# State-space tables built ahead of the expert loop, parked in DRAM and reloaded

## The reference

```python
abr = mag * jnp.cos(li * dt)            # Abar, 64 groups x 64 states
abi = mag * jnp.sin(li * dt)
bbar_re = qr[..., None] * br - qi[..., None] * bim
bbar_im = qr[..., None] * bim + qi[..., None] * br
bu_re = jnp.einsum('blgh,gph->blgp', u, bbar_re)
bu_im = jnp.einsum('blgh,gph->blgp', u, bbar_im)
...                                     # x_t = Abar x_{t-1} + Bbar u_t
y = (jnp.einsum('ghp,blgp->blgh', c_re, xr)
     - jnp.einsum('ghp,blgp->blgh', c_im, xi))
y = y + d * h                           # then GELU and a gated output projection
```

## Time and profile before

| what | value |
|---|---|
| device time, median of 3 runs | 2999.33 us (2990.56 to 3006.65) |
| the profiled execution's own time | 2996.05 us |
| its span, first to last instruction | 2994.3 us |
| busy: PE, DVE, ACT, POOL | 89%, 68%, 45%, 9% of the span |
| matmuls' chain (share of the span on PE) | 77% |
| granted TensorE clock, mean | 0.934 of full speed |
| expert loop, 407 to 1558 us | PE 1138.5 of 1151 us busy, clock 0.99, 364 GB/s |
| 1558 to 1908 us | PE busy in about half |

### The profile page before, as it was taken

How to read it: one execution, slowest core, us unless ns; L and a number is a source line. 1 busy time by engine, 2 the same in 40 slices (tenths; PEclk the granted TensorE clock), 3 DMA queues, 4 the chain that set the end, 5 groups by cost and what they waited for, 6 DMA issues and landing times.

```text
span 2994.3 us, 34160 instructions
## 1 busy us (share of the span) xinstructions
PE 2655.8 (89%) x12072; PEld 2135.3 (71%) x12072; DVE 2021.4 (68%) x1948; ACT 1335.2 (45%) x1316; POOL 282.6 (9%) x337
## 2 busy tenths in 40 slices
PE   6988589999999999999974772789999999799997
PEld 4766468888888888888852362668888778588885
DVE  5764578999989999999959935656653354533433
ACT  4331257777777777777742221232222232322221
POOL 1230230000000000000007300001100000000000
PEclk9998589999999999999986866889999999999998
DMA  6741589999999999999963066317754423233332
GB/s 235 251 132 43 189 289 377 375 376 379 376 376 377 377 377 376 377 377 378 377 190 123 0 70 56 95 53 217 231 148 111 108 70 82 57 94 97 103 97 67
DMA packets 368686, 634.84 MB, mean 212 GB/s; under 512 B 45004, under 2 KB 238740, under 8 KB 368436
## 3 DMA queue, kind: packets, MB, share of 16 engines
q1 hardware_dynamic: 346196, 539.16, 54.5%
q0 software_dynamic: 17296, 76.03, 7.5%
q10 hardware_dynamic: 5136, 18.88, 1.5%
HBM read 609.97 MB, written 24.58 MB: 212 GB/s over the span
## 4 chain that ended last, share of the span: by engine, by line
PE 77%; DVE 12%; DMA 4%; ACT 2%; SPq 2%; issue 1%; POOL 1%; DVEq 0%; POOLq 0%; ACTq 0%
PE bank L2035 35%; PE bank L2235 11%; PE bank L2236 11%; PE bank L2241 11%; SPq L507 2%; PE bank L2023 1%; PE bank L2011 1%; PE bank L2018 1%; PE bank L1860 1%; DMA ring<-in_w_ada 1%; DVE work L1597 1%; DMA cb<-in_w_ada 1%; DMA ring<-k_dram 1%; DVE cb L1217 1%; DVE work L1596 1%
## 5 line engine op out<-in xcount | busy, mean ns | idle before, releaser
L1487 DVE TENSOR_TENSOR slot_lo<-ring,slot_hi 128x2048 fp32r<-128x2048 f32 x384 | 864.8, 2287 | 113.7 <-ACT slot_hi L909 113.6
L909 ACT ACTIVATE slot_hi<-ring 128x2048 fp32r<-128x2048 f32 x384 | 736.4, 1920 | 304.5 <-PE bank L2035 274.9
L2035 PE MATMUL bank<-slot_hi,xs_hi 128*128 128x512 f32 x1024 | 325.3, 399 | 0.0
L2035 PE MATMUL bank<-slot_hi,xs_lo 128*128 128x512 f32 x1024 | 317.5, 391 | 0.0
L2235 PE MATMUL bank<-h_hi,fin_hi 128*128 128x512 f32 x704 | 277.6, 394 | 22.6 <-ACT h_hi L1043 22.1
L2236 PE MATMUL bank<-h_hi,fin_lo 128*128 128x512 f32 x704 | 276.0, 392 | 0.0
L2035 PE MATMUL bank<-slot_lo,xs_hi 128*128 128x512 f32 x1024 | 275.7, 391 | 0.0
L2035 PEld LDWEIGHTS bank<-slot_hi,xs_hi 128*128 128x128 f32 x1024 | 188.8, 189 | 59.8 <-issue 23.9
L2035 PEld LDWEIGHTS bank<-slot_hi,xs_lo 128*128 128x128 f32 x1024 | 193.4, 189 | 41.5
L2035 PEld LDWEIGHTS bank<-slot_lo,xs_hi 128*128 128x128 f32 x1024 | 193.4, 189 | 40.4
L1084 ACT ACTIVATE fin_hi<-rows 128x1024 fp32r<-128x1024 f32 x88 | 88.2, 1052 | 220.8 <-DMA rows<-in_w_ffn_in 220.8
(11 more groups left out here) (431 smaller groups left out, 4297.9 us busy)
## 6 DMA issues: line engine op xcount, KB each, us to landing
ring<-in_expert_w_gate_up SPq DMA_DIRECT2D x256, 1024.0 KB, 7.0
ring<-in_expert_w_down SPq DMA_DIRECT2D x128, 1024.0 KB, 6.7
rows<-in_w_ffn_in SPq DMA_DIRECT2D x88, 512.0 KB, 5.0
work<-in_w_ada POOLq DMA_DIRECT2D x64, 384.0 KB, 4.0
cb<-in_w_ada POOLq DMA_DIRECT2D x48, 384.0 KB, 4.6
y_dram<-cb ACTq DMA_DIRECT2D x32, 512.0 KB, 7.2
work<-in_w_ffn_out SPq DMA_DIRECT2D x8, 1408.0 KB, 7.0
rows<-in_w_ffn_out SPq DMA_DIRECT2D x8, 1408.0 KB, 6.9
```

What stands on the lines that cost most here:

```text
L909: act.activation(hi_of(e, j), slot[q], ACT.Copy).then_inc(s_slot_hi, 1)
L1487: tt(slot_lo[:, q], slot[q], whole(hi_of(e, j)), ALU.subtract).then_inc(s_slot_lo, 1)
L2035: last = mm(ps[banks + n], x[:, k, :], (lo if lower else hi)[:, k, 512 * n:512 * (n + 1)], start=(begins and lower == 0 and k == 0 and x i ...
```

## The change

The tables are built in front of the expert loop. `m_b` and the powers are computed on POOL (the powers in three doubling steps with up to 256 columns, from `early_power`), C is loaded and transposed for a first time (`c_early`, `c_first`), PE transposes `m_b` behind the logits and forms the lag products in two halves around the token ids, ACT copies the transposes into free places (`m_w_parts`) and stores them to `m_w_dram`, and SP stores the lag table behind expert 0's last weights. Behind the loop `m_t` and `m_w` are loaded from DRAM. Waits are added for this: DVE waits for the slabs and for the zeros before its routing work, ACT for the powers and the stores, SP holds back expert 0's four down slots until the lag products are made (they use the same place in `ring`), and PE waits for the copies of the lag products before it uses that bank again. C is loaded a second time behind the loop, for `m_c`.

```diff
-COLS_PLE = COLS_ROUTE + 2 + KD
-COLS_XT = COLS_PLE + G // 4 + KD
+COLS_MB = COLS_ROUTE + G // 4
+COLS_PLE = COLS_MB + 2 + KD
+COLS_XT = COLS_PLE + KD
...
+        m_b = ring[:, 16384:24576].rearrange("p (g v h) -> p g v h", g=G, v=CH)
+        slab = [m_b[:, :, v, :] for v in range(CH)]
+        i_bbar = slab[0]
+        c_early = ring[:, 16384:17408].rearrange("p (t two n) -> p t two n", t=8, two=2)
+        c_first = work[:, 9216:10240].rearrange("p (g h) -> p g h", g=G)
+        m_w_parts = [(0, ca[:].rearrange("p k t -> p (k t)")), (4096, nat[:, 2048:4096]), (6144, work[:, 7680:9216]),
+                     (7680, work[:, 2048:2560])]
...
+            def load_c(rows_of, r):
+                for d in range(2):
+                    part = (r + d) % 2
+                    load(rows_of[:, :, d, :], a[f"ssm_c_{('re', 'im')[part]}_2"][0].rearrange("(t g) h n -> (g h) t n", t=8), s_c_in)
+            kd = k_dram.rearrange("h g v o -> h g (v o)")
+            sp.wait_ge(s_score_sb, HEADS * NT)
+            load_c(c_early, 0)
+            sp.wait_ge(s_power_ok, 1)
+            sp.wait_ge(s_y_ps, HEADS)
+            sp.wait_ge(s_b_in, 32)
+            for r in range(2):
+                for d in range(2):
+                    load(b_in[r][NS * d:NS * (d + 1)], b_dram[(r + d) % 2], s_b_in)
+            sp.dma_start(kd[:, :, 0:(CH - 1) * GC],
+                         k_zero.unsqueeze(1).broadcast_to([GC, G, (CH - 1) * GC])).then_inc(s_k_out, 16)
...
-            sp.wait_ge(s_hn_stored, 16)
+            sp.wait_ge(s_act_stored, 16)
             sp.wait_ge(s_cols_ready, COLS_ROUTE)
             for half in range(2):
                 load(bias_rows[E * half:E * (half + 1), :], a["expert_b_gate_up"][0], s_bias_in)
             load(down_bias, a["expert_b_down"][0], s_bias_in)
+            sp.wait_ge(s_k_ps, 1)
             for q in range(8, 12):
                 load_slot(q, 0)
+            sp.wait_ge(s_k_sb, 2)
+            for v in range(CH):
+                sp.dma_start(k_dram[:, :, 2 * CH - 2 - v, :], k_sb[GC * v:GC * (v + 1), :, :]).then_inc(s_k_out, 16)
             load_up(1, 1, 1)
...
+            sp.wait_ge(s_k_out, 16 * (CH + 1))
+            sp.wait_ge(s_more_done, 1)
+            for v in range(CH):
+                load(m_t[GC * v:GC * (v + 1), :, :], kd[:, :, (CH - 1 - v) * GC:(2 * CH - 1 - v) * GC], s_t_in)
+            sp.wait_ge(s_pgate_ready, 2 * NT)
+            sp.wait_ge(s_act_stored, 16 * len(m_w_parts) + 16)
+            load(m_w, m_w_dram.rearrange("p (g m) -> p g m", g=G), s_t_in)
...
-            kd = k_dram.rearrange("h g v o -> h g (v o)")
-            sp.wait_ge(s_k_sb, 3)
-            for v in range(CH):
-                sp.dma_start(k_dram[:, :, 2 * CH - 2 - v, :], k_sb[GC * v:GC * (v + 1), :, :]).then_inc(s_k_out, 16)
-            sp.dma_start(kd[:, :, 0:(CH - 1) * GC],
-                         k_zero.unsqueeze(1).broadcast_to([GC, G, (CH - 1) * GC])).then_inc(s_k_out, 16)
-            sp.wait_ge(s_k_out, 16 * (CH + 1))
-            for v in range(CH):
-                load(m_t[GC * v:GC * (v + 1), :, :], kd[:, :, (CH - 1 - v) * GC:(2 * CH - 1 - v) * GC], s_t_in)
...
+            pool.wait_ge(s_score_sb, 6 * NT + 1)
+            pool.wait_ge(s_par_ok, 1)
+            step(pool.memset(k_zero, 0.0))
+            for r in range(2):
+                step(pool.tensor_copy(early_power[r][:, 0], par[:, r, :]))
+            for n in (1, 2, 4):
+                xr, xi = [v[:, 0:n] for v in early_power]
+                ar, ai = [v[:, n - 1:n].broadcast_to([P, n, G]) for v in early_power]
+                t0, t1 = [v[:, 0:n * G].rearrange("p (v g) -> p v g", v=n) for v in power_t]
+                step(ptt(t0, xr, ar, ALU.mult))
+                step(ptt(t1, xi, ai, ALU.mult))
+                step(ptt(early_power[0][:, n:2 * n], t0, t1, ALU.subtract))
+                step(ptt(t0, xr, ai, ALU.mult))
+                step(ptt(t1, xi, ar, ALU.mult))
+                step(ptt(early_power[1][:, n:2 * n], t0, t1, ALU.add))
+            pool.sem_inc(s_power_ok, 1)
+            def wide_g(v):
+                return v.unsqueeze(2).broadcast_to([P, G, GC])
+            def turned(dst, x, y, z, w, op):
+                step(ptt(s5_ta[0], x, wide_g(z), ALU.mult))
+                step(ptt(s5_ta[1], y, wide_g(w), ALU.mult))
+                step(ptt(dst, s5_ta[0], s5_ta[1], op))
+            def power_slab(v):
+                turned(slab[v], slab[CH - 1], i_bbar, early_power[0][:, CH - 2 - v], early_power[1][:, CH - 2 - v], ALU.add)
+            def bbar_slabs():
+                pool.wait_ge(s_b_in, 96)
+                pool.wait_ge(s_ct_ps, 2)
+                sign = sm[:, 192:193]
+                step(pool.tensor_scalar(sign, token[:, 0:1], NS - 0.5, 2.0, ALU.is_gt, ALU.mult))
+                step(pool.tensor_scalar(sign, sign, -1.0, None, ALU.add))
+                step(pool.tensor_scalar(turn[:], par[:, 2:4, :], sign, None, ALU.mult))
+                turned(slab[CH - 1], b_in[0], b_in[1], par[:, 2, :], turn[:, 1, :], ALU.add)
+            pool.wait_ge(s_ret_ready, 1)
+            bbar_slabs()
+            turned(i_bbar, b_in[1], b_in[0], turn[:, 0, :], par[:, 3, :], ALU.subtract)
+            for v in range(CH - 2, -1, -1):
+                power_slab(v)
+            pool.sem_inc(s_b_ready, 1)
+            pool.wait_ge(s_nat_ready, 2 * NT)
+            for r in range(2):
+                step(pool.tensor_copy(power[:, r], early_power[r]))
+            pool.sem_inc(s_power_ok, 1)
             pool.wait_ge(s_bias_in, 48)
             up_bias = bias_rows.rearrange("e (f two) -> e f two", two=2)[:, :, 1]
             pool.tensor_scalar(up_bias, up_bias, 1.0, None, ALU.add).then_inc(s_bias_one, 1)
             pool.wait_ge(s_route_ok, 1)
-            pool.wait_ge(s_hn_stored, 16)
+            pool.wait_ge(s_act_stored, 16)
+            pool.wait_ge(s_act_stored, 16 * len(m_w_parts) + 16)
...
-            pool.wait_ge(s_b_in, 96)
-            step(pool.tensor_scalar(b_in[1][0:NS], b_in[1][0:NS], -1.0, None, ALU.mult))
-            pool.wait_ge(s_more_done, 1)
-            bbar = m_b[:, :, CH - 1, :]
-            turned(bbar, b_in[0], b_in[1], par[:, 2, :], par[:, 3, :], ALU.add)
-            turned(i_bbar, b_in[1], b_in[0], par[:, 2, :], par[:, 3, :], ALU.subtract)
-            pool.sem_inc(s_b_ready, 1)
-            for v in range(CH - 2, -1, -1):
-                turned(m_b[:, :, v, :], bbar, i_bbar, power[:, 0, CH - 2 - v, :], power[:, 1, CH - 2 - v, :], ALU.add)
-            pool.sem_inc(s_b_ready, 1)
-            pool.wait_ge(s_pproj_ready, 2 * NT)
-            pool.memset(k_zero, 0.0).then_inc(s_k_sb, 1)
...
+            act.wait_ge(s_log_ps, 1)
+            act.wait_ge(s_act_stored, 16)
+            act.wait_ge(s_power_ok, 2)
+            for first, part in m_w_parts:
+                for at in range(0, part.shape[1], 512):
+                    column(part[:, at:at + 512])
+                act.wait_ge(s_cols_taken, COLS_ROUTE + (first + part.shape[1]) // 512)
+                act.dma_start(m_w_dram[:, first:first + part.shape[1]], part).then_inc(s_act_stored, 16)
...
+            act.wait_ge(s_act_stored, 16 * len(m_w_parts) + 16)
             for j in range(LEAD):
                 split_high(0, j)
+            act.wait_ge(s_k_ps, 1)
+            for n in range(2):
+                act.activation(k_sb[:, GP * n:GP * (n + 1), :], ps[n].rearrange("p (g h) -> p g h", g=GP), ACT.Copy).then_inc(s_k_sb, 1)
...
+            dve.wait_ge(s_b_ready, 1)
+            dve.wait_ge(s_k_out, 16)
...
-                if b == 0:
-                    dve.wait_ge(s_k_out, 16 * (CH + 1))
...
+            pe.wait_ge(s_c_in, 32)
+            for q in range(2):
+                c_transposes(c_early, q, 6 + q)
...
+            pe.wait_ge(s_b_ready, 1)
+            for q in range(G // 4):
+                column([m_b[:, 4 * q + j].rearrange("p v h -> p (v h)") for j in range(4)])
+            def lag_kernels(half):
+                for g in range(GP * half, GP * (half + 1)):
+                    last = mm(ps[half][:, GC * (g % GP):GC * (g % GP + 1)], m_b[:, g].rearrange("p v h -> p (v h)"), c_first[:, g, :], start=True, stop=True)
+                return last
...
+            lag_kernels(0)
             for n in range(NT * TOPK):
                 pe.wait_ge(s_slot_hot, 2 * n + 2)
                 last = mm(ps[6][:, 0:TILES], row_hot[:, n, :], tile_token[:, n, :], start=(n == 0), stop=(n == NT * TOPK - 1))
             last.then_inc(s_ids_ps, 1)
+            lag_kernels(1).then_inc(s_k_ps, 1)
...
+            pe.wait_ge(s_k_sb, 2)
...
-            pe.wait_ge(s_pgate_act, 2 * NT)
-            for g in range(G):
-                last = mm(ps[g // GP][:, GC * (g % GP):GC * (g % GP + 1)], m_b[:, g].rearrange("p s h -> p (s h)"),
-                          s5c[0][:, g, :], start=True, stop=True)
-            last.then_inc(s_k_ps, 1)
...
-            pe.wait_ge(s_t_in, 16 * CH)
```

88 lines of the change are left out of this document (32 added, 56 removed).

## The result

The changed kernel takes 2951.64 us (median of 4 runs, 2943.95 to 2954.05); the kernel before, 3001.27 us in the same session (4 runs, 2990.56 to 3006.65). The ratio is 0.9835, 95% interval 0.9801 to 0.9868: faster by 1.65%, some 50 us. The profiled execution took 2949.81 us with a span of 2948.1, against 2996.05 and 2994.3. The forecast was 2952.

What follows compares the result with a forecast made beforehand. TensorE (PE) bounds the expert loop, so only the stretches around it count: -69.4 behind, +31.5 in front, -8 between the first experts, -45.9 us from 2996.05 to 2950; forecast 2952, range 2930 to 2980.

Steps and rivals of the forecast that it cites:

- the table's transposes: Behind the loop: the table's 64 transposes leave PE, net 1.0 us gained after 2.5 given back for a lower clock.
- Behind the loop, contention, -34.3: Behind the loop: without POOL's 27 operations DVE's work runs clean and the last projection pair ends 34.3 us earlier.
- Lag table's return, -34.1: Behind the loop: waits for the lag table's stores and return from DRAM go, first GELU starts 34.1 us earlier.
- m_w reload, nothing: Behind the loop: 4 MB of m_w come back in 11 us under 60 us of cover, so no cost.
- Slabs in front, +19.2: In front of the loop: POOL's 27 slab operations hold DVE's port, rows ready 19.2 us later; bounds 6 and 30.
- the 10 to 12 among my signs: Sign of being right: twelve tiny DVE operations take 10 to 12 us in front of the logits.
- the early lock is cheap: Rival: in front, POOL's operations slip between PE-paced ones; front costs 17 instead of 31.5, total 2937 us; chance 0.18.
- Columns between logits and ranks, +5.0: In front: 16 transpose groups and ACT copies delay DVE's reading of the ranks by 5.0 us; bounds 2 and 12.
- Second half of the lag products, +7.3: In front of expert 0: the second half of 64 lag products holds up PE, 7.3 us; bounds 3 and 14.
- Between experts 0 and 1, -8: Token tile 1's gather no longer queues behind the powers, less later weight loads: 8 us gained; bounds 0 and 11.
- ACT waiting for weights in experts 0 to 2: Sign of being wrong: in the loop's first experts, ACT waits for weights; no size given.
- the second: Rival: front costs 44, the gather's 8 us gain is lost, late loads stall ACT's splits; 2972 us, chance 0.20.

Runs made afterwards that it cites:

- experiment 3: The kernel before without POOL's 27 table operations behind the loop, all else kept: 2966.92 us, ratio 0.9901.
- experiment 5: The changed kernel with the lag table's eight loads put back behind the u loads on SP, its stores left early: 2966.13 us, ratio 0.9899.
- Experiment 2: The changed kernel without POOL's 27 table operations in front of the loop: 2931.53 us, ratio 0.9787.
- experiment 7: The changed kernel with POOL pausing behind the fourth of seven power slabs until the hn rows are scaled: 2938.06 us, ratio 0.9800.
- experiment 1: The changed kernel run once more, unaltered: 2948.90 us, ratio 0.9843 to the kernel before.
- experiment 4: The kernel before with only POOL's 44 power operations moved in front, from behind the first gather: 2985.17 us, ratio 0.9961.
- experiment 6: The changed kernel with the eight lag-table stores behind expert 1's eight weight loads on SP, instead of ahead: 2940.65 us, ratio 0.9813.

## Why the prediction was right

Every mechanism in the sum that the rows can tell held; one term, the table's transposes, they can't tell. The clear misses in size lie in front of the loop, and two of them are terms put too high. Terms by the table, measured as the changed kernel's two profiles against the kernel before:

- *Behind the loop, contention, -34.3:* measured -35.1 and -35.6, and experiment 3 has it alone with -35.5. Right.
- *Table's transposes, +1.0 of gain:* not to be told from the 67 to 74 us that this stretch takes in any kernel. The three profiles with the transposes behind the loop average 71.6 us, the ten without 70.6, which is too little beside that spread. Open.
- *Lag table's return, -34.1:* -34.7 twice. Right in mechanism and size; what is late next is the second recurrence, as said: DVE ends it and waits only 0.92 us for PE. Only my later split of it was off (experiment 5).
- *m_w reload, nothing:* no wait for it anywhere; SP issues it at 1694.32 and it is needed from 1773 on.
- *Slabs in front, +19.2:* rows ready 18.9 and 18.2 us later against the ring pass. Right; the twelve tiny operations cost 9.8 and 10.6 (9.6 in the sum), the scalings 2.0 (3.5), what lies before them 7.1 and 5.6 (6.1). With 12.2 and 13.0 us the tiny ones were slightly above the 10 to 12 among my signs. Experiment 2 takes the operations away and gets the time back, experiment 7 gets back 9.0 at expert 0 by a pause. The rival "the early lock is cheap" fell with this.
- *Columns between logits and ranks, +5.0:* 20.0 and 19.2 instead of 16.3 us, 2.9 to 3.7. A little too high: ACT's exponential and bias copy queued as I said, but DVE waited less for them than I took.
- *Second half of the lag products, +7.3:* 26.15 instead of 20.9 us from the one-hot rows to expert 0, 5.2. Too high by 2, and half of that is a slip: the parts as I wrote them, 12.7 + 1.1 - 2.5 - 5, make 6.3, not 7.3. The first half cost nothing, as said: ranks to one-hot rows is 9.14 us in both.
- *Colder PE at the logits:* I had no term for it; 2.4 us in one profile (20.6 instead of 18.2 us from rows to logits), 0 in the other. The granted clock there was 0.59 and 0.68 (experiment 1).
- *Between experts 0 and 1, -8:* -7.0 and -7.3. The two parts were each too small and nearly cancel: alone the gather is worth 10.4 us (experiment 4), where I took 9, and the loading queue takes back 3.3 us (experiment 6), where I took 1. "ACT waiting for weights in experts 0 to 2" was among my signs of being wrong. It happened, 3.37 us once, and only made the gain smaller; as a sign that the prediction is wrong it was badly chosen.

In front of expert 0 that makes 26.3 to 30.2 us where the sum had 31.5. The front was neither cheap (17), as the first rival had it, nor dear (44), as the second had it; of the second's mechanism, ACT late in its splits, 3.3 us were there, at expert 1 (experiment 6). The profiled execution came 46.2 us under the one before and the sum said 45.9, but part of that agreement is luck. The sum had nothing for the ring pass, which came 4.3 us later by chance, nor for the stretch behind the GELU, 1.9 us longer in this profile; the stretch "to product", shorter by 5.9 us where the sum had 1.0, made up for them. By the medians the difference is 48.6 to 49.6 us. So what was mis-sized is the front's 31.5 us, by 1.3 to 5.2.
